# The head block of a two-layer diffusion trunk: rows, turns, shifts and splits in another order

## The reference, cut to what matters

```python
def rms_norm(x, g):
    x32 = x.astype(jnp.float32)
    y = x32 * lax.rsqrt(jnp.mean(x32 * x32, axis=-1, keepdims=True) + EPS)
    return (y * g.astype(jnp.float32)).astype(x.dtype)

def layer(x, cond, p, l, angles, ctx):
    mod = jax.nn.silu(cond) @ p['w_mod'][l] + p['b_mod'][l]        # 1024 -> 6 * 1024
    sh1, sc1, g1, sh2, sc2, g2 = jnp.split(mod, 6, axis=-1)
    h = rms_norm(x, p['norm1'][l]) * (1.0 + sc1) + sh1
    mixed, ctx_out = token_mixers(h, p, l, angles, ctx)            # begins with h @ p['w_in'][l]
    ...
```

## Time and profile before

| | us |
|---|---|
| median of three runs | 2462.07 (2461.62 to 2463.23) |
| span of the profiled execution | 2464.2 |
| PE busy | 2354.2 (96%) |
| DVE busy | 1498.5 (61%) |
| ACT busy | 1074.1 (44%) |
| POOL busy | 218.1 (9%) |

### The profile page before, as it was taken

One profiled execution on the slowest core, in us unless ns is written; L12 is line 12 of the kernel. 1 busy time (PEld: TensorE's weight loads), 2 busy tenths in 40 slices (PEclk: granted clock), 3 DMA queues, 4 the chain that ended last, 5 costly groups with the idle time before them and its releaser, 6 DMA issues. The chain is left out here.

```text
span 2464.2 us, 41036 instructions
## 1 busy us (share of the span) xinstructions
PE 2354.2 (96%) x16478; PEld 2181.3 (89%) x16478; DVE 1498.5 (61%) x2400; ACT 1074.1 (44%) x2129; POOL 218.1 (9%) x176
## 2 busy tenths in 40 slices
PE   6989989999999999999999899898999999999998
PEld 5867867789999899999998678677999989999998
DVE  3334656766665773755653446586776568557473
ACT  3533346744442552533435233576444335335252
POOL 1241000000002100000134110000000040000000
PEclk8989999999999999999999999999999999999999
DMA  8235223022225122332231441301222342323222
GB/s 244 88 99 182 70 87 129 27 70 77 89 83 184 48 86 69 86 103 69 78 102 54 148 144 38 102 1 43 78 78 78 111 129 77 96 69 96 59 82 82
DMA packets 248747, 224.03 MB, mean 91 GB/s; under 512 B 9040, under 2 KB 234384, under 8 KB 248048
## 3 DMA queue, kind: packets, MB, share of 16 engines
q1 hardware_dynamic: 242240, 218.59, 28.2%
q10 hardware_dynamic: 5808, 2.17, 0.4%
q0 software_dynamic: 512, 0.66, 0.3%
HBM read 211.70 MB, written 9.70 MB: 90 GB/s over the span
## 5 line engine op out<-in xcount | busy, mean ns | idle before, releaser
L2267 ACT ACTIVATE ring_high<-raw 128x512 fp32r<-128x512 f32 (+1 forms) x278 | 158.1, 609 | 254.0 <-PE ps L2626 146.6
L2411 DVE TENSOR_TENSOR ring_low<-raw,ring_high 128x512 fp32r<-128x512 f32 (+1 forms) x278 | 204.9, 763 | 74.1 <-ACT ring_high L2267 70.0
L2699 PE MATMUL ps<-hH,ring_low 128*128 128x320 f32 x640 | 197.9, 309 | 0.3
L2699 PE MATMUL ps<-hL,ring_high 128*128 128x320 f32 x640 | 197.8, 309 | 0.0
L2699 PE MATMUL ps<-hH,ring_high 128*128 128x320 f32 x640 | 197.8, 309 | 0.0
L1482 DVE SCALAR_TENSOR_TENSOR xT<-ps,mod,xT 128x512 f32<-128x512 f32 (+1 forms) x128 | 64.0, 546 | 189.2 <-PE ps L2626 189.2
L344 PE MATMUL ps<-wH,hL 128*128 128x512 f32 (+1 forms) x460 | 174.5, 379 | 4.8 <-DVEq L1038 3.6
L344 PE MATMUL ps<-wH,hH 128*128 128x512 f32 (+1 forms) x460 | 171.6, 373 | 0.0
L2626 PE MATMUL ps<-gH,ring_low 128*128 128x320 f32 x704 | 160.9, 310 | 0.3 <-DVE xT L1482 0.3
L2626 PE MATMUL ps<-gL,ring_high 128*128 128x320 f32 x704 | 160.4, 309 | 0.0
L2626 PE MATMUL ps<-gH,ring_high 128*128 128x320 f32 x704 | 160.4, 309 | 0.0
(11 more groups left out here) (381 smaller groups left out, 6307.8 us busy)
## 6 DMA issues: line engine op xcount, KB each, us to landing
raw<-in_w_in SPq DMA_DIRECT2D x56, 1024.0 KB, 5.2
raw<-in_w_ffn_in SPq DMA_DIRECT2D x88, 512.0 KB, 5.1
gmod<-in_w_mod SPq DMA_DIRECT2D x16, 1024.0 KB, 6.4
modw<-in_w_mod SPq DMA_DIRECT2D x16, 1024.0 KB, 5.3
raw<-in_w_ffn_out SPq DMA_DIRECT2D x16, 1024.0 KB, 5.3
b_raw<-in_w_branch SPq DMA_DIRECT2D x22, 512.0 KB, 3.9
head_w<-in_w_mod SPq DMA_DIRECT2D x8, 1024.0 KB, 12.3
raw<-in_w_out SPq DMA_DIRECT2D x8, 1024.0 KB, 6.3
```

The costliest lines, as they stand in the source:

```text
L2267: nc.scalar.activation(ring_block(m.ring_high, b, src.shape[1], src.shape[2]), src, ACT.Copy).then_inc(m.sem("w_high"), 1)
L2411: nc.vector.tensor_tensor(ring_block(m.ring_low, b, nk, cols), src, ring_block(m.ring_high, b, nk, cols).bitcast(F32), ALU.subtract).then_ ...
L2699: last = nc.tensor.matmul(m.ps[:, plan.banks[n, 0][BANK[what]], 0:HALF], w[:, k, :], a[:, k, :], start=(first and k == 0 and q == 0), stop ...
```

## The change

- c and c_ctx are loaded as sixteen rows of 512 bytes into c_rows; PE turns them (one more transpose, bank 6, counter `cond_turned`), and ACT applies Silu from there.
- POOL issues the fourteen small parameter loads only when the eighth modulation slab has landed (`mod_loaded7`).
- turn(p) writes into bank 6 or 7, from which the row of the same pair has been copied, and no longer waits for the normalized tiles. mod(2) and mod(3) wait for `affine` in place of `mod_rows`.
- ACT does rows(p) directly ahead of pair p and not one pair ahead; within a pair the odd tile's shift comes first, then the high part of the even tile, then that of the odd one.
- DVE normalizes tiles 0 to 3, does the modulation and the shift of pair 0, then normalizes tile 4, splits the first slab, splits pair 0, normalizes tiles 5 to 7, and goes on with pair 1.

The arithmetic is the same. The diff:

```diff
--- before.py
+++ after.py
@@ -138,7 +138,6 @@
             return t
 
         self.cst = place("cst", [P, K_COLS])
-        self.sc = place("sc", [P, KT, 2])
         self.sc32 = place("sc32", [P, KT, MG])
         self.sel = place("sel", [P, 2])
         self.mod = place("mod", [P, 48, 2])
@@ -167,6 +166,7 @@
         self.mbr = at("mbr", [DEPTH * 48, P], 102400)
         self.nw_rows = at("nw_rows", [DEPTH * 2 * KT, P], 102400 + 512)
         self.lpw = at("lpw", [P, DEPTH, 2, HD], 102400 + 1024)
+        self.c_rows = at("c_rows", [2 * KT, P], 102400 + 2048)
 
         self.xrow = at("xrow", [P, TT, D], 20480)
 
@@ -1707,6 +1707,7 @@
             small = m.sem("small_params")
             pool.memset(m.sc32[:, :, :], 0.0).then_inc(m.sem("sc_zero"), 1)
             pool.dma_start(m.sel[:, :], d["const_sel"]).then_inc(m.sem("selector"), 16)
+            pool.wait_ge(m.sem("mod_loaded7"), 16)
             for L in range(DEPTH):
                 pool.dma_start(m.lp[:, L, :], d["diff_lambda"][L:L + 1, :, :].rearrange("a b c -> (a b c)").
                                partition_broadcast(P)).then_inc(small, 16)
@@ -1723,10 +1724,8 @@
 
         @block.scalar
         def _(act):
-            act.dma_start(m.sc[:, :, 0:1], d["c"].rearrange("a (k p) -> p k a", p=P),
-                          allow_slow_non_contiguous=True).then_inc(m.sem("cond"), 16)
-            act.dma_start(m.sc[:, :, 1:2], d["c_ctx"].rearrange("(a k p) -> p k a", p=P, a=1),
-                          allow_slow_non_contiguous=True).then_inc(m.sem("cond"), 16)
+            act.dma_start(m.c_rows[0:KT, :], d["c"].rearrange("a (k p) -> (a k) p", p=P)).then_inc(m.sem("cond"), 16)
+            act.dma_start(m.c_rows[KT:2 * KT, :], d["c_ctx"].rearrange("(k p) -> k p", p=P)).then_inc(m.sem("cond"), 16)
             act.dma_start(m.nw_rows[0:DEPTH * KT, :],
                           d["norm1"].rearrange("l (k p) -> (l k) p", p=P)).then_inc(m.sem("bias_rows"), 16)
             act.dma_start(m.nw_rows[DEPTH * KT:2 * DEPTH * KT, :],
@@ -1741,9 +1740,10 @@
             act.wait_ge(m.sem("row_squared"), TT)
             nc.scalar.activation(m.n_st[:, 0:5], m.n_st[:, 0:5], ACT.Sqrt, scale=1.0 / D,
                                  bias=m.cst[:, K_LAM + 4:K_LAM + 5]).then_inc(m.sem("std"), 1)
-            act.wait_ge(m.sem("cond"), 32)
+            act.wait_ge(m.sem("cond_turned"), 1)
             act.wait_ge(m.sem("sc_zero"), 1)
-            nc.scalar.activation(m.sc32[:, :, 0:2], m.sc[:, :, :], ACT.Silu).then_inc(m.sem("silu"), 1)
+            nc.scalar.activation(m.sc32[:, :, 0:2], m.ps[:, 6, 0:2 * KT].rearrange("p (c k) -> p k c", c=2), ACT.Silu
+                                 ).then_inc(m.sem("silu"), 1)
 
             def rows(p):
                 act.wait_ge(m.sem("slab_used"), 2 * p + 2)
@@ -1754,19 +1754,18 @@
             rows(0)
             high_slab(nc, m, act, 0, slabs[0], at_load[0])
             for p in range(4):
-                if p + 1 < 4:
-                    rows(p + 1)
+                if p:
+                    rows(p)
                 act.wait_ge(m.sem("affine"), p + 1)
-                for k in (2 * p, 2 * p + 1):
-                    if k % 2:
-                        for c, seg in enumerate(segments(m.x_n[:, k, :])):
-                            ins = nc.scalar.activation(seg, seg, ACT.Identity, scale=m.aff[:, 0, k, c:c + 1],
-                                                       bias=m.mod[:, k, c:c + 1])
-                        ins.then_inc(m.sem("shifted_act"), 1)
-                        act.wait_ge(m.sem("shifted_act"), p + 1)
-                    else:
-                        act.wait_ge(m.sem("shifted"), p + 1)
-                    nc.scalar.activation(m.hH[:, k, :], m.x_n[:, k, :], ACT.Copy).then_inc(m.sem("h_high"), 1)
+                odd = m.x_n[:, 2 * p + 1, :]
+                for c, seg in enumerate(segments(odd)):
+                    ins = nc.scalar.activation(seg, seg, ACT.Identity, scale=m.aff[:, 0, 2 * p + 1, c:c + 1],
+                                               bias=m.mod[:, 2 * p + 1, c:c + 1])
+                ins.then_inc(m.sem("shifted_act"), 1)
+                act.wait_ge(m.sem("shifted"), p + 1)
+                nc.scalar.activation(m.hH[:, 2 * p, :], m.x_n[:, 2 * p, :], ACT.Copy).then_inc(m.sem("h_high"), 1)
+                act.wait_ge(m.sem("shifted_act"), p + 1)
+                nc.scalar.activation(m.hH[:, 2 * p + 1, :], odd, ACT.Copy).then_inc(m.sem("h_high"), 1)
             ahead = slabs_ahead(slabs)
             for n, slab in enumerate(slabs):
                 if n == 1:
@@ -1810,15 +1809,17 @@
             dve.wait_ge(m.sem("rstd_spread"), 1)
             dve.wait_ge(m.sem("copied"), TT)
             spread = m.ps[:, 4:6, :].rearrange("p b c -> p (b c)")[:, 0:T]
-            for k in range(KT):
-                nc.vector.tensor_tensor(m.x_n[:, k, :], m.xT[:, k, :], spread, ALU.mult).then_inc(m.sem("x_normed"), 1)
-            low_slab(nc, m, dve, 0, slabs[0])
+            def x_norm(ks):
+                for k in ks:
+                    nc.vector.tensor_tensor(m.x_n[:, k, :], m.xT[:, k, :], spread, ALU.mult).then_inc(m.sem("x_normed"), 1)
+
+            x_norm(range(4))
             dve.wait_ge(*bias)
             for p in range(4):
                 dve.wait_ge(m.sem("mod_turned"), p + 1)
                 for part in range(2):
                     t = 8 * part + 2 * p
-                    src = m.ps[:, 4 + p % 2, 4 * part:4 * part + 4].rearrange("p (t c) -> p t c", c=2)
+                    src = m.ps[:, 6 + p % 2, 4 * part:4 * part + 4].rearrange("p (t c) -> p t c", c=2)
                     done = order.step(nc.vector.tensor_tensor(
                         m.mod[:, t:t + 2, :], src, m.mb[:, 0, t:t + 2].unsqueeze(2).broadcast_to([P, 2, 2]), ALU.add))
                 dve.wait_ge(*done)
@@ -1830,10 +1831,15 @@
                 dve.wait_ge(m.sem("affine"), p + 1)
                 dve.wait_ge(m.sem("x_normed"), 2 * p + 1)
                 shift(nc.vector, m, 0, 2 * p, m.x_n[:, 2 * p, :]).then_inc(m.sem("shifted"), 1)
+                if p == 0:
+                    x_norm((4,))
+                    low_slab(nc, m, dve, 0, slabs[0])
                 for k in (2 * p, 2 * p + 1):
                     dve.wait_ge(m.sem("h_high"), k + 1)
                     nc.vector.tensor_tensor(m.hL[:, k, :], m.x_n[:, k, :], m.hH[:, k, :].bitcast(F32), ALU.subtract
                                             ).then_inc(m.sem("h_low"), 1)
+                if p == 0:
+                    x_norm((5, 6, 7))
             low_slab(nc, m, dve, 1, slabs[1])
             dve.wait_ge(m.sem("small_params"), 2 * 7 * 16)
             lp = m.lp[:, :, :].rearrange("p l (a b c) -> p l a b c", a=2, b=2)
@@ -1878,6 +1884,9 @@
             nc.tensor.transpose(m.ps[:, 7, 64:64 + nb], m.mbr[:, :], m.cst[0:nb, K_ID:K_ID + nb])
             nc.tensor.transpose(m.ps[:, 7, 0:4 * KT], m.nw_rows[:, :], m.cst[0:4 * KT, K_ID:K_ID + 4 * KT]
                                 ).then_inc(m.sem("bias_turned"), 1)
+            pe.wait_ge(m.sem("cond"), 32)
+            nc.tensor.transpose(m.ps[:, 6, 0:2 * KT], m.c_rows[:, :], m.cst[0:2 * KT, K_ID:K_ID + 2 * KT]
+                                ).then_inc(m.sem("cond_turned"), 1)
             pe.wait_ge(m.sem("rstd"), 1)
             spread_rstd(nc, m, 4, TILE_AT).then_inc(m.sem("rstd_spread"), 1)
             pe.wait_ge(m.sem("silu"), 1)
@@ -1885,7 +1894,7 @@
 
             def mod(p):
                 if p >= 2:
-                    pe.wait_ge(m.sem("mod_rows"), p - 1)
+                    pe.wait_ge(m.sem("affine"), p - 1)
                 if p == 1:
                     pe.wait_ge(m.sem("x_normed"), 1)
                 for part in range(2):
@@ -1894,10 +1903,8 @@
 
             def turn(p):
                 pe.wait_ge(m.sem("mod_rows"), p + 1)
-                if p < 2:
-                    pe.wait_ge(m.sem("x_normed"), KT)
                 for t in range(4):
-                    last = nc.tensor.matmul(m.ps[:, 4 + p % 2, 2 * t:2 * t + 2],
+                    last = nc.tensor.matmul(m.ps[:, 6 + p % 2, 2 * t:2 * t + 2],
                                             m.head_row[:, p % 2, t * P:(t + 1) * P], m.sel[:, :], start=True, stop=True)
                 last.then_inc(m.sem("mod_turned"), 1)
```

## The result

The changed kernel takes 2449.0 us in the median (2447.1 to 2452.1) against 2462.7 for the kernel before in the same session: ratio 0.9946, 95% interval 0.9932 to 0.9960. That is 13.6 us faster, 0.54%. The forecast was 2450.2, with a range of 2446 to 2455.

A forecast was written before the change was run, and what follows sets the result against it. TensorE, busy 2354.2 of 2464.2 us, was taken as the bound, so only its idle or low-clock time in the head could go: 9.8 + 2.1 = 11.9 us, from 2462.07 to 2450.2, range 2446 to 2455.

The forecast's parts named there:

- The bound and the walk back: Head block: TensorE bounds; starting the second w_in slab (68.87 us) earlier moves the kernel's end by the same amount.
- The transfers: Head loads: without element-wise and early software-queue packets, the fourth modulation slab lands at 26.2 us, before 35.8.
- The trail of 3.3 us: Fourth modulation slab: counted as landed 3.3 us after its bytes, some engines being behind; expected to shrink under 1 us.
- rival 1: Head loads: the slab stream itself causes the 3.3 us trail, which stays; gain 9.1 us, time 2453.0; chance 0.17.
- The first chain: Kernel start to first product: transposes, rstd, mod, turn and splits; first product at 30.4 us against 40.20, 9.8 us earlier.
- From the first product to the second slab: Rest of the head: two waits of 0.43 us and one of 1.23 go, 28.67 becomes 26.6; 2.1 us more.
- the clock's dips: Between first product and second slab: TensorE's two shorter falls to the lower clock were assumed to stay the same.
- Two of my signs: Trace signs in the head: granted clock 0.50 in two short later places; no TensorE wait on low at the second slab.
- Rival 2: Head: TensorE has fewer gaps and stays at its upper clock; gain 16.4 us, time 2445.7; chance 0.08.
- Sum: Whole kernel: 9.8 + 2.1 = 11.9 us faster, 0.5%, giving 2450.2 against the median of 2462.07.
- 3: Behind the head: a later transfer or fixed-time load swallows the gain; time 2460 to 2462; chance 0.04.
- 4: Small parameters land too late, stalling VectorE, ScalarE and then TensorE; slower, 2467; costs from about 58 us; chance 0.03.

The follow-up runs named there:

- e12_later: Changed kernel with the small parameters issued behind tile_done (about 54 us) in place of the eighth slab; 2465.5 us, ratio 1.0014 to the kernel before.
- e1_rows: Kernel before with only the conditioning vectors loaded as rows and turned on PE; 2462.0 us against 2462.6, ratio 0.9999.
- e10_cols: Changed kernel with c and c_ctx loaded element by element again, without the added transpose; 2447.6 us, ratio 0.9943 to the kernel before.
- e2_late: Kernel before with only POOL's small parameter loads waiting for the eighth modulation slab; 2451.2 us against 2462.6, ratio 0.9960.
- e9_mid: Changed kernel with the small parameters issued after the second modulation slab (near 17 us) in place of the eighth; 2453.1 us, ratio 0.9967 to the kernel before.
- e3_loads: Kernel before with both load changes (conditioning rows and late small parameters), old order of work; 2451.4 us, ratio 0.9959.
- e8_act: Changed kernel with ScalarE's old order, rows(p+1) again ahead of pair p's shift and high parts; 2455.4 us, ratio 0.9973 to the kernel before.
- e11_fill: Changed kernel with TensorE's order moved: dense(0) between the halves of mod(1), dense(1) ahead of turn(2); 2447.4 us, ratio 0.9941 to the kernel before.

## Why the prediction was right

**The bound and the walk back.** Right. The head's end was the second slab, and what it gained, 13.8 us, came out at the end, 13.9. One such pair could be chance, since what lies behind scatters by 5 us. But in every run except e12_later, whose wait lies behind the second slab, the time gained in the median and the shift of the second slab against 68.87 agree within 2 us (order alone 4.3 and 5.3, late parameters 11.4 and 10.2, the changed kernel again 12.9 and 14.2).

**The transfers.** The date was right (fourth slab 26.2 forecast, 26.30 measured), its reason only in part. I put the late slabs down to single elements and software packets together; e1_rows and e10_cols show that the elements did nothing, e2_late that the small parameters on the software queue did all. The row on which I leaned, 17.2 us until c_ctx landed, showed a victim and not a culprit: the same load landed after 10.7 us in e10_cols, with the parameters gone. The trail of 3.3 us shrank to 1.2, a little more than the 1 us that I allowed: the changed kernel had moved 8.06 MB by 25.1 us (321 GB/s on average), and the slab released TensorE at 26.3. That settles rival 1 for this slab. That single engines of the sixteen were behind was my inference; no view here shows them one by one. The eighth slab came at 39.65 where I wrote 38, which cost nothing. Here the Trainium skill's rule on non-contiguous last dimensions (DMA: Bandwidth & Descriptors, Rules for kernel authors) gave me a cause too many: the packets are as it says, and at 8 KB they don't matter. The other rule that I took from the Trainium skill (same page, Issuing engines are not separate DMA queues), that all queues share the same engines, held: in e9_mid the price came back wherever slabs were still wanted, and in the changed kernel it is hidden only because nothing of that time is wanted soon: the second slab of w_in is split from 50.8 us on.

**The first chain.** The spread rstd ended at 15.6 and not 19.0. Only the first of the transposes took the 1.94 us per eight that I had reckoned for all (1.97); the last sixteen took 2.19 together, so the transposes of the rows ended at 12.5 and not 15.1, and the spread itself took 1.38 and not 2.50. turn(0) took 1.05, and hL of tile 1 was ready at 26.1, where I had tile 0 at 28.9 to 29.7. All this slack, 3.3 us of it ahead of mod(1), went into TensorE's wait for the slabs. The first product, 30.68 against 30.4 forecast, was set by the fourth slab, half of mod(1) and turn(1) at the lower clock (1.93 and 1.87 us), and the row copy between them (0.72). e3_loads adds what I had only assumed: the old order would have reached it as early.

**From the first product to the second slab.** The mis-sized term: I gave 2.1 us, it was 4.3 (28.67 to 24.4). The waits were sized right, 2.2 us by the starts of the products: the two of 0.43 us went with the small gaps beside them (1.1 together), and of the 1.23 us 1.1 went. A wait for the low part is left (0.38 us on the weight load), since dense(2) and dense(3) now take 7.5 us and not 8.8. The other 2.1 us are the clock, which I had taken as unchanged. Without its dip dense(1) is 1.6 us shorter, and dense(2) with dense(3) 1.5; dense(0) is 1.0 longer, since it starts earlier in a stretch at the lower level. What I had left standing were the clock's dips, "because the row copy and the short turn products that stood ahead of each dip stay". They stay, and the dips went: in no profile did they bring a dip without a further wait, for hL or for the row, and even with one a dip does not come each time. That the time still came out within the forecast is because the two errors, 0.3 us too much ahead of the first product and 2.2 too little behind it, are small beside the sum. Two of my signs did not come: the two short places at 0.50, and no wait on low at the second slab. Rival 2 was half true, for the two later dips and not for the first product. In e8_act waits of 1.5 us bring both dips back, in e11_fill they don't.

**Sum.** 9.5 + 4.3 = 13.8 us in place of 9.8 + 2.1 = 11.9. The split between the edits, from the runs: late parameters 11.4 us alone, order 4.3 alone, rows nothing; together 13.6 in the first comparison and 12.9 in the second. The parts add up to more than the whole, 15.7, but each has an interval of 2 to 3 us to either side; in the shift of the second slab they give 10.2 + 5.3 = 15.5 against 13.8 and 14.2. Part of the overlap shows: the late parameters alone already leave one dip of the clock in place of two.

**The rivals.** 3 did not occur. 4 was sound and nearer than its 0.03 suggests: the last of the parameters landed 0.1 us before VectorE used them (I had 57 against 58, so 1 us), and some 0.9 us more were free before TensorE would have waited. POOL's start 15 us later made the kernel slower than before.

## What to carry to other kernels

Small broadcast loads on the software queue that nobody needs soon should start behind the large loads that someone waits for, and ahead of their own first use by more than their landing time; here one wait on an idle engine was worth 11 us, and the same wait 15 us later cost all of it. The margin is to be read from the load that lands last, not from the median of a line: here that is 0.1 us in place of 1.7. Of several suspicious loads in one window, remove them one at a time before one is blamed: the ugliest descriptor pattern was free. An earlier start of a stage is worth nothing unless the idle time in front of it is filled and not moved.

## What I had not expected of the hardware

- 14 software-queue loads with 0.66 MB in 512 packets held up 1 MB slabs by 9.5 us at the start and by 4.8 us in mid-stream (share of the sixteen engines 6.8 and 4.9 us). Why the start costs more than its share stays open; e1_rows rules out the element-wise packets. Whether the price is that of the software queue or of spreading each load over all partitions is open too, since no run issued the same loads in another way.
- 2048 four-byte packets beside the slabs: ratio 0.9999 (0.9990 to 1.0008).
- The granted clock reads 1.00 for the first 20 us of the changed kernel, yet eight transposes took 1.94 us at 4.91 us, and sixteen took 2.19 us at 10.32. The record seems not to show the lower level ahead of the first change.
- Idle times of 0.43 us for hL, beside 0.72 us for the row, can go with a fall of the clock to its 1.2 GHz level (mean 0.66 in 50 to 55 us). Of eight such waits in four kernels five were followed by a dip; without a wait for hL or a longer one for the row, seven profiles of seven show none; and e11_fill shows none behind waits of 1.58 and 1.87 us. What decides is open, and so is the share of the short turn products.
